# A change to the second block's attentions in a two-block transformer kernel: pairs of heads in one accumulator, another order on ScalarE, one joined head loop

## The reference

```
proj = rmsnorm(h) @ w_in[l];  main, mq = proj[..., :768], proj[..., 768:]
layer 0: main_out = pool_mixer(main)      # four groups, window means over 2, 4, 8, 16 tokens
layer 1: main_out = swa_sink_attention(rmsnorm(main), k_shared, v_shared, sinks)
         # 12 query heads of width 64, 4 key/value heads, window 128, causal, position bias,
         # a learned sink in each softmax's denominator
mem_out = memory_attention(rmsnorm(mq), mk, mv)          # 4 heads of width 64, 256 memory rows
h = h + concat([main_out, mem_out]) @ w_out[l]
h = h + relu(rmsnorm(h) @ w_up[l])**2 @ w_down[l]
```

## Time and profile before

| | us |
|---|---|
| median of 3 runs | 1760.87 (1757.15 to 1761.19) |
| the profiled execution, its own time | 1758.72 |
| its span, first to last instruction | 1756.9 |
| TensorE busy | 1525.0 (87%) |
| VectorE busy | 1062.1 (60%) |
| ScalarE busy | 754.9 (43%) |
| GpSimd busy | 276.7 (16%) |
| mean granted TensorE clock | 0.982 of full |

### The profile page before, as it was taken

One profiled execution on the slowest core, in us unless ns is written; L12 is line 12 of the kernel. 1 busy time (PEld: TensorE's weight loads), 2 busy tenths in 40 slices (PEclk: granted clock), 3 DMA queues, 4 the chain that ended last, 5 costly groups with the idle time before them and its releaser, 6 DMA issues.

```text
span 1756.9 us, 20895 instructions
## 1 busy us (share of the span) xinstructions
PE 1525.0 (87%) x8008; PEld 1145.7 (65%) x8008; DVE 1062.1 (60%) x1938; ACT 754.9 (43%) x1395; POOL 276.7 (16%) x326
## 2 busy tenths in 40 slices
PE   7999999998998877777777687777999999789999
PEld 7998989977883322222222232256899878679987
DVE  5468646764486667666677766456544556754454
ACT  5544555443443333334333333244455346545532
POOL 0000000000023343334333343303000002000000
PEclk9999999999999999999999999999999999899999
DMA  6744344453479999999999999942455653124563
GB/s 247 247 177 144 145 144 148 168 171 114 144 292 418 421 422 422 421 421 421 421 416 422 422 406 422 422 171 73 168 171 189 192 174 100 45 88 177 192 191 120
DMA packets 71043, 442.11 MB, mean 252 GB/s; under 512 B 7031, under 2 KB 9343, under 8 KB 25504
## 3 DMA queue, kind: packets, MB, share of 16 engines
q0 software_dynamic: 36864, 268.45, 36.9%
q1 hardware_dynamic: 30208, 163.59, 27.1%
q10 hardware_dynamic: 3872, 8.75, 1.4%
HBM read 439.70 MB, written 2.63 MB: 252 GB/s over the span
## 4 chain that ended last, share of the span: by engine, by line
PE 58%; DMA 24%; DVE 9%; ACT 5%; issue 2%; POOL 1%; ACTq 0%; SPq 0%; DVEq 0%; POOLq 0%
PE banks L1070 28%; DMA arena<-experts,xn 24%; PE banks L1099 16%; PE banks L1352 7%; DVE w_lo L1495 2%; DVE arena L1888 2%; PE banks L1196 1%; PE banks L1183 1%; PE banks L1136 1%; ACT xn L884 1%; ACT xn L888 1%; ACT w_hi L608 1%; ACT op_hi L633 1%; ACT xn L877 1%; ACT arena L687 0%
## 5 line engine op out<-in xcount | busy, mean ns | idle before, releaser
L1352 PE MATMUL banks<-arena,xn 128*128 128x512 f32 x1024 | 483.7, 618 | 157.4 <-ACT xn L888 157.4
L1495 DVE TENSOR_TENSOR w_lo<-raw,w_hi 128x2048 fp32r<-128x2048 f32 x154 | 352.3, 2290 | 261.6 <-PE banks L1070 131.7
L1352 PEld LDWEIGHTS banks<-arena,xn 128*128 128x128 f32 x1024 | 189.4, 194 | 449.6 <-ACT xn L888 256.0
L1888 DVE CUSTOM_DVE_ANT_0 arena<-arena,banks 128x1024 f32<-128x1024 f32 x256 | 312.1, 1219 | 213.6 <-DMA arena<-experts,xn 213.2
L608 ACT ACTIVATE w_hi<-raw 128x2048 fp32r<-128x2048 f32 x154 | 293.3, 1911 | 162.3 <-PE banks L1099 131.6
L546 POOL DMA_INDIRECT arena<-experts,xn x256 | 243.3, 950 | 435.9 <-PE banks L1352 383.8
L1070 PE MATMUL banks<-op_hi,w_hi 128*128 128x256 f32 x1520 | 220.5, 287 | 2.3 <-ACT op_hi L633 2.3
L1070 PE MATMUL banks<-op_hi,w_lo 128*128 128x256 f32 x1520 | 214.1, 284 | 7.8 <-DVE w_lo L1495 7.8
L1070 PE MATMUL banks<-op_lo,w_hi 128*128 128x256 f32 x1520 | 214.2, 284 | 0.0
L877 ACT ACTIVATE xn<-xn,stat 128x2 f32<-128x2 f32 x128 | 37.8, 295 | 395.1 <-DVE xn L1888 395.1
L1070 PEld LDWEIGHTS banks<-op_hi,w_hi 128*128 128x128 f32 x1520 | 198.2, 193 | 6.9 <-ACT op_hi L633 4.3
(11 more groups left out here) (225 smaller groups left out, 1154.1 us busy)
## 6 DMA issues: line engine op xcount, KB each, us to landing
raw<-wstream SPq DMA_DIRECT2D x154, 1024.0 KB, 5.1
arena<-experts,xn POOLq DMA_INDIRECT x256, 12.6
xn<-mem_in ACTq DMA_DIRECT2D x2, 1024.0 KB, 4.8
scratch<-scratch ACTq DMA_DIRECT2D x1, 1536.0 KB
x<-x_in SPq DMA_DIRECT2D x2, 512.0 KB, 4.3
arena<-scratch ACTq DMA_DIRECT2D x1, 1024.0 KB, 7.4
arena<-keys_in ACTq DMA_DIRECT2D x1, 1024.0 KB, 5.9
out_dram<-x SPq DMA_DIRECT2D x4, 256.0 KB, 2.0
```

What stands on the lines that cost most here:

```text
L1352: mm = pe.matmul(sums[:, n, :], diag[:, s, :], rows[:, s, D + n * CW:D + (n + 1) * CW], start=(at == 0), stop=(at == PAIRS - 1), skip_grou ...
L1495: dve.tensor_tensor(w_lo[:, n % LO, :, :], raw[:, n % RAW, :, :], w_hi[:, n % HI, :, :].bitcast(F32), ALU.subtract).then_inc(lo_ready, 1)
L1888: dve.tensor_tensor_reduce(u, u, token_rows[k // PAIRS][:, :, :], 1.0, 0.0, ALU.mult, ALU.add, dots[:, s:s + 1]).then_inc(dot_ready, 1)
```

## The change

There are five parts.

1. Two windowed heads share an accumulator. `v_swa` becomes `[P, TB, 2, 2, P]`: for each value head a tile with zeros to its right and one with zeros to its left (two memsets and two copies of half the width in place of one copy). The value products of heads 2p and 2p+1 add into one projection bank, and K is done once for the pair, on 128 partitions.
2. In the second layer's two loops ScalarE does C(i) ahead of E(i+2) in place of behind it.
3. The loops are joined: S, M and E of the first two memory heads are issued in the windowed loop at heads 10 and 11.
4. The last square root (memory queries) is gone from ScalarE: it adds 1e-6 and copies, and POOL raises to -0.5. VectorE only negates.
5. Pooling tile 5 goes from POOL to VectorE, behind M(3) of the first memory attention; the splits of blocks (0,0) and (0,1) follow it.

The diff, cut to its core:

```diff
 plan():
+        if c == "inb" and i:
+            for p in range(SWA_TILES):
+                place(lin, lin_uses, ("O", "swa", p))
 ...
+            elif after:
+                m("S", after, i + lag - items)
-            if i:
+            if i and kind != "swa":
                 m("O", kind, i - 1)
             m("T", kind, i)
-    attention("swa", SWA_HEADS, 1, 2, [("qr", 2)], [(), (), [("qr", 3)]])
-    attention("memb", MEM_HEADS, 1, 2)
+    attention("swa", SWA_HEADS, 1, 2, [("qr", 2)], [(), (), [("qr", 3)]], after="memb")
+    attention("memb", MEM_HEADS, 1, 2, begun=True)
-        v_swa = part(4608, TB, S)
+        v_swa = part(5632, TB, 2, 2, P)
 gpsimd:
-            for t in range(3, SWA_TILES):
+            for t in (3, 4):
 ...
+            misc_emptied(pool, ("qr", 3))
+            pool.tensor_tensor(query_inv[:, 3, :], query_root[:, 3, :], small[:, 14:15].broadcast_to([P, 8]), ALU.pow)\
+                .then_inc(memory_roots, 1)
 scalar:
-                if i >= 2:
+                if i >= 2 and kind == "swa":
+                    act.wait_ge(swa_out, i - 1)
+                elif i >= 2:
                     wait_misc(act, ("O", kind, i - 2))
 ...
                 for i in range(items):
+                    if kind in ("swa", "memb"):
+                        turned(kind, i)
                     if i + lag < items:
                         for g in range(group):
                             free_prob(kind, i + lag, group)
                             exps(kind, (i + lag) * group + g)
+                    elif after:
+                        free_prob(kind, i + lag, group)
+                        exps(after, i + lag - items)
 ...
-                    turned(kind, i)
+                    if kind not in ("swa", "memb"):
+                        turned(kind, i)
 ...
-            copy_lin(("kvb", 1), v_swa[:, :, :])
+            product(("kvb", 1))
+            act.wait_ge(v_zeros, 1)
+            v = lin_bank(("kvb", 1)).rearrange("p (t a c d) -> p t a c d", t=TB, a=2, c=2)
+            for c in range(2):
+                e = act.activation(v_swa[:, :, :, c, c * HD:(c + 1) * HD], v[:, :, :, c, :], ACT.Copy)
+            empty_lin(e, ("kvb", 1))
+            def memory_means():
+                key = ("qr", 3)
+                wait_misc(act, key)
+                empty_misc(act.activation(query_root[:, 3, :], misc_bank(key)[:, 0:8], ACT.Identity,
+                                          bias=small[:, 9:10]), key)
 tensor:
+                    if kind == "swa":
+                        key = ("O", "swa", i // 2)
+                        if i % 2 == 0:
+                            lin_bank_free(key)
+                        for kb in range(2):
+                            mm = pe.matmul(lin_bank(key)[:, kb * P:S], values(i)[0](kb),
+                                           prob_t[:, (ITEM0[kind] + i) % 2, kb * S:(kb + 1) * S - kb * P],
+                                           start=(i % 2 == 0 and kb == 0), stop=(i % 2 == 1 and kb == 1))
+                        mm.then_inc(swa_out, 1)
+                        return
 ...
+                    elif after:
+                        s(i + lag - items, *after)
-                      lambda u: [lambda kb: v_swa[:, kb, (u // 6) * P:(u // 6 + 1) * P]],
+                      lambda u: [lambda kb: v_swa[:, kb, u // 6, u % 2, :]],
 vector:
+                    if kind == "swa":
+                        if i % 2:
+                            key = ("O", "swa", i // 2)
+                            dve.wait_ge(swa_out, i + 1)
+                            src, t = lin_bank(key)[:, 0:S], i // 2
+                            do(dve.tensor_copy(op_hi[:, 1, t, :], src))
+                            empty_lin(dve.tensor_tensor(op_lo[:, 1, t, :], src, op_hi[:, 1, t, :].bitcast(F32),
+                                                        ALU.subtract), key)
+                        return
 ...
+            def last_window():
+                lin_emptied(dve, ("ina", 3))
+                windows(SWA_TILES - 1)
+                pool_low(0, 0)
+                pool_low(0, 1)
-                      [next_low_parts, pool_lows((0, 0), (0, 1)), pool_lows((0, 2), (1, 0)), pool_lows((1, 1), (1, 2))])
+                      [next_low_parts, last_window, pool_lows((0, 2), (1, 0)), pool_lows((1, 1), (1, 2))])
 ...
+            do(dve.memset(v_swa[:, :, :, 0, HD:P], 0.0))
+            dve.memset(v_swa[:, :, :, 1, 0:HD], 0.0).then_inc(v_zeros, 1)
 ...
+            def memory_inverses():
+                low_parts(LAST[("inb", 3)] + 2)
+                dve.wait_ge(memory_roots, 1)
+                do(dve.tensor_scalar(query_neg[:, 3, :], query_inv[:, 3, :], -1.0, None, ALU.mult))
```

More of the change, by code:

```diff
@@ L135, in norm, with attention @@
             m("xT", n, j)
-    def attention(kind, items, group, lag, between=(), fill=()):
-        for i in range(min(lag, items)):
+    def attention(kind, items, group, lag, between=(), fill=(), after=None, begun=False):
+        for i in range(0 if begun else min(lag, items)):
             for g in range(group):
@@ L345, in build @@
         late_windows = sem("late_windows")
+        memory_roots = sem("memory_roots")
+        swa_out = sem("swa_out")
+        v_zeros = sem("v_zeros")
         query_gains = sem("query_gains")
@@ L707, in free_prob, with attention @@
                     wait_misc(act, ("T", kind, j))
-            def attention(kind, items, group, lag, fill=(), between=None):
+            def attention(kind, items, group, lag, fill=(), between=None, after=None, begun=False):
                 start = halves[0]
-                for i in range(min(lag, items)):
+                for i in range(0 if begun else min(lag, items)):
                     for g in range(group):
@@ L1011, in _ @@
             query_roots(("qr", 1), 1)
-            attention("swa", SWA_HEADS, 1, 2, [None, None, lambda: query_roots(("qr", 3), 3)], last_queries)
-            attention("memb", MEM_HEADS, 1, 2)
+            attention("swa", SWA_HEADS, 1, 2, [None, None, memory_means], last_queries, after="memb")
+            attention("memb", MEM_HEADS, 1, 2, begun=True)
             squares_and_rows("mlpb", "outb", 0)
@@ L1172, in normed, with attention, s @@
                 return dict(hi_made=made(norm_hi), lo_made=made(norm_lo))
-            def attention(kind, items, group, lag, scores, values, fill=(), between=None):
-                def s(u):
+            def attention(kind, items, group, lag, scores, values, fill=(), between=None, after=None, begun=False):
+                def s(u, kind=kind, scores=scores):
                     b = fill_misc(("S", kind, u))
@@ L1452, in _, with memory_scores @@
             point(pe, "k_swa")
+            def memory_scores(h, qb):
+                if h == 0 and qb == 0:
+                    misc_emptied(pe, ("qr", 3))
+                return [(q_swa[:, h % 2, SWA_TILES + h // 2, qb * P:(qb + 1) * P], memk[:, 1, h // 2, :])]
             attention("swa", SWA_HEADS, 1, 2,
@@ L1455, in _ @@
                                      (slopes[:, u, qb, :], alibi[:, qb, :])],
-                      lambda u: [lambda kb: v_swa[:, kb, (u // 6) * P:(u // 6 + 1) * P]],
-                      [None, None, lambda: query_means_b(3)], last_half)
-            misc_emptied(pe, ("qr", 3))
-            attention("memb", MEM_HEADS, 1, 2,
-                      lambda h, qb: [(q_swa[:, h % 2, SWA_TILES + h // 2, qb * P:(qb + 1) * P],
-                                      memk[:, 1, h // 2, :])],
-                      lambda h: [lambda kb: memv[:, 1, kb, (h // 2) * P:(h // 2 + 1) * P]])
-            for u in range(SWA_HEADS):
-                misc_emptied(pe, ("O", "swa", u))
+                      lambda u: [lambda kb: v_swa[:, kb, u // 6, u % 2, :]],
+                      [None, None, lambda: query_means_b(3)], last_half, after=("memb", memory_scores))
+            attention("memb", MEM_HEADS, 1, 2, memory_scores,
+                      lambda h: [lambda kb: memv[:, 1, kb, (h // 2) * P:(h // 2 + 1) * P]], begun=True)
+            for p in range(SWA_TILES):
+                lin_emptied(pe, ("O", "swa", p))
             for h in range(MEM_HEADS):
@@ L1654, in normalise, with attention @@
                                       ALU.mult).then_inc(p_ready, 1)
-            def attention(kind, items, group, lag, extra, dst, fill=(), lows=()):
-                for i in range(min(lag, items)):
+            def attention(kind, items, group, lag, extra, dst, fill=(), lows=(), after=None, begun=False):
+                for i in range(0 if begun else min(lag, items)):
                     for g in range(group):
@@ L1684, in attention @@
                             maxima(kind, u, **extra(u))
+                    elif after:
+                        wait_misc(dve, ("T", kind, i + lag - 4))
+                        maxima(after, i + lag - items)
                     if i < len(lows):
@@ L1992, in windows @@
```

(8 more changed lines are left out.)

4 lines of the change are left out of this document (2 added, 2 removed).

## The result

| | us |
|---|---|
| changed kernel, median of 6 runs | 1743.9 (1741.1 to 1748.0) |
| kernel before, beside it, median of 6 | 1758.7 (1754.8 to 1761.2) |
| ratio, with its 95% interval | 0.9917 (0.9899 to 0.9936) |
| profiled execution, its span | 1741.14, 1739.3 |
| forecast, range | 1744.9, 1739.5 to 1752 |

The change saves 14.8 us by the medians, where 16.0 were forecast.

The account below looks back on a forecast made before the run. Head stages were taken as round trips between engines, VectorE nearest to full. 3.7 + 3.0 + 4.7 + 1.1 - 0.3 + 3.8 = 16.0 us saved gave 1742.7, or 1744.9 us on the runs' scale; range 1739.5 to 1752.

Parts of the forecast that it names:

- What bounds the kernel: Second layer's head stages: a round trip between engines, VectorE nearest to full; a microsecond saved there is saved at the end.
- The loop: Steady windowed heads, N(4) to N(11): K once per pair lowers VectorE's work; 3.0 us gain, bounds 0 to 3.7.
- about nothing: Steady loop under the new bank rules: S(i+3)'s wait for E(i+1) was judged to cost about nothing.
- Rival E: Windowed loop: VectorE's work isn't the limit, 2.95 us per head stays; 3.0 less gain, 1747.9 us; chance 12%.
- The first heads: N(1) to N(4): table loads and a bank wait go, N(4) starts earlier; 3.7 us gain, bounds 1.5 to 4.5.
- The joint: End of N(11) to end of memory head 0's N: 8.5 us becomes 3.8; 4.7 gain, bounds 3.5 to 5.5.
- The memory heads: Memory head 0's N to the output projection: 11.9 us becomes 10.8; 1.1 gain, between 0 and 2.
- Copies and memsets: Ahead of the loop: two copies in place of one cost 0 to 0.6 us, taken as -0.3.
- Pooling: Layer 0, tile 5 on VectorE: block (1,0) starts earlier despite half collision; 3.8 us gain, bounds 0.5 to 6.3.
- rival D: Layer 0's pooling: VectorE and POOL collide fully, gain 0.5 in place of 3.8 us, 1748.2 us; chance 12%.
- Rival B: Shortened loop: TensorE's clock falls for half of seven steps, costing 4.9 us, 1749.8 us; chance 15%.
- rival C: Clock stays low from N(1) through the memory heads and beside the pooling: 4.6 us slower, 1765.5 us; chance 3%.

Follow-up runs that it names:

- e4: Changed kernel with K done twice for each pair (same values written again); median 1749.47 us, ratio 0.995.
- e2: Changed kernel with part 2 undone, ScalarE doing E(i+2) ahead of C(i) again; median 1748.12 us, ratio 0.9945.
- e10: Part 1 alone on the kernel before, the other four parts undone; median 1753.76 us, ratio 0.9975.
- e5: Part 2 alone on the kernel before, C(i) ahead of E(i+2); median 1758.5 us against 1759.02, ratio 1.0002.
- e11: Changed kernel with part 4 undone, the memory queries' square root on ScalarE again; median 1742.76 us, ratio 0.991.
- e3: Changed kernel with part 3 undone, windowed and memory heads as two loops again; median 1746.71 us, ratio 0.993.
- e8: Changed kernel with K of the last windowed pair moved behind N and M of memory head 0; median 1742.24 us, ratio 0.991.
- e9: Changed kernel with that K moved later and the first heads' `low_parts` moved behind the memory heads; median 1741.59 us, ratio 0.991.
- the changed kernel's second profile: The changed kernel run again without edits, beside later runs; median 1746.43 us, ratio 0.9929.

## Why the prediction held, step by step

**What bounds the kernel.** The reading that a microsecond saved in the stages is one saved at the end held: the stage gains sum to 14.6, the medians differ by 14.8, and from the projection to the end both profiles took 209.6. The time came out 1.0 from the forecast, nearer than the saving (14.8 for 16.0), because the kernel before, measured beside it, was 2.1 lower than the median that the forecast started from. That is luck, and so is part of the sum: the loop gave 0.9 more than forecast, the first heads 1.45 and the pooling 0.9 less.

**The loop** (3.0 forecast, 3.93 measured). VectorE is the bound, as said, and e4 shows it. The forecast without hand-offs was 17.1, and 16.72 came: a pair took the 4.78 worked out, and the first and the last step were shorter, 2.67 and 2.61 for 2.78. So the 0.5 that I kept for hand-offs was not needed. What failed is the step that gave the gain to part 1 alone. It compared busy times of single engines and found S's wait for E "about nothing". It did not follow the ring through ScalarE's list, where C stood behind E: 5.73 us per pair in e2 and in the middle of e10. Rival E had the right suspicion (the loop keeps 2.95, C comes through two engines), and its own counter, "C moves ahead", is half of the answer. Part 2 opens this ring, but alone it closes the one through E's bank, 3.20 per head in e5; part 1, which moves O out of those banks, opens that one and lowers VectorE's own work besides. With both rings open VectorE's list is what is left. So neither part shows without the other (20.09 and 21.20 alone).

**The first heads** (3.7, 2.25). The term that was mis-sized is the clock at S(4), which I had in the bounds (1.5 to 4.5) and at zero in the sum: it took 1.66. Where it did not occur (e11), the stretch was 9.81, and 13.49 - 9.81 is the forecast's 3.7. The kernel before had run this stretch at 0.87, so at like clocks the new order is worth 2.25. Counting the two table loads among the causes was wrong in attribution: e11 has them and loses 0.23.

**The joint** (4.7, 4.75). Length and chain as worked out. But the forecast compared a stretch of the changed kernel at full clock with one of before at 0.68, and put all of it on the joining, which is worth 1.9 (e3). Another 1.9 belong to the clock and the order of C together (e5); no run parts these two. So the near match of 4.7 and 4.75 is partly luck.

**The memory heads** (1.1, 0.86). It is part 2's: 11.05 to 11.07 in every profile with C first but three, 11.92 in those without (before, e2, e10). The three are e4, at a clock of 0.84, and e8 and e9, which have K of the last pair in this stretch.

**Copies and memsets** (-0.3, -0.1). From the pooling stage to N(1), where no stretch was slow, 261.09 against 261.01 in e5, which lacks them. The two memsets took 0.27 each.

**Pooling** (3.8, 2.9). The collision was sized at half and was larger: tile 5 took 5.9 us, not 5.1, and POOL's tile 4 beside it 1.0 more than alone. The splits behind it kept their length (0.86 for two, 0.87 before). It was not rival D's 8 us. The Trainium skill, GPSIMD Engine Reference, section Specifications, says that POOL shares its SBUF interfaces with VectorE and contends with instructions of VectorE that have two SBUF inputs or run in a two-port mode. The trace agrees for the two-input ones (0.42 became 0.63 and 0.80), but not each was stretched: the additions that VectorE began together with a copy of POOL kept 0.42. Copies, with one input, were caught as well: 0.60, 0.60 and 0.71 for two, four and eight columns, while that of one column kept 0.14 beside POOL's addition. In which mode these copies ran the trace does not tell.

**Rival B and rival C** (the clock falls in the loop, or everywhere). Neither occurred: 1.00 in loop, joint and memory heads. In e10 the clock was 0.87 in the loop and 0.61 in the joint, so the danger was real for half of this change. The Trainium skill, TensorE: Matmul & The Clock Gate, section A second HAM failure mode: psum-queue depth-cycling, which the prediction named for B, says that short pauses between groups of products, as banks cycle, can make the clock swing. No run here shows it: e10's middle pairs, with waits of 0.2 to 0.4 us in front of O in every head, ran at 0.99 and 1.00, as the changed kernel's loop did at 1.00, and e10's clock was low where TensorE had waited 1.5 us and more.

**The prices of rivals B and C.** C's own terms add to 4.1 + 0.3 = 4.4, where 4.6 was written, and B took 1.75 for the lower level where its row gives 634/379 = 1.67. Neither changes the outcome.

**The rest of the spans' 17.6.** The stages of these two profiles give 14.1. The other 3.5 lie in stretches that no part touches: 1.85 ahead of the pooling stage, whose cause is open, and 1.6 between it and N(1). There every profile has about 261.1, 262.6 or 264.3, steps of 1.6. One such step, the transposes ahead of layer 1's projections, in the kernel before:

```profile
1438.30:1450.40 12.10, 11.45 (x82) 11.28 (x83) 9.51 (x20) 6.86 (x17) 0.00 (x0) 0.86 0.31 108
```

The same 82 products take 11.45 us busy here at a granted 0.86, and 9.82 in the changed kernel at 1.00 (the second row of its windows above). Both occur with the same kernel: the changed kernel's second profile has 264.3 in the larger stretch. Such steps may well be the 2.5 us between its own two medians, 1743.9 and 1746.4, but that is not shown, since only one execution of each was profiled. What decides whether such a stretch comes slow was not found.

## What to carry to other kernels

In a loop that goes head by head over in-order engines, compare each engine's work per round with the longest ring of waits through all the lists and banks, over as many heads as banks and buffers span. An instruction that stands behind another on a half-idle engine can close a ring that hides a gain elsewhere, and moving it can close the next ring, so two edits may be worth 3.9 us together and 1.4 apart. A mean per head over a short loop can hide a ring, so read the steps one by one. Before crediting a stretch to an edit, read its granted clock on both sides. An elementwise piece moved to the neighbour of a busy engine costs more than its own time: here 5.9 us for 3.5, and 1.0 to the other.

## What was new about the hardware

- GpSimd's power over 128x8 took 1.65 us in both profiles quoted, against 0.54 to 0.72 for one or two columns.
- VectorE and POOL beside each other take turns, and the shortest instructions pay: a copy of four columns took 0.60 on VectorE, where one or two columns alone take 0.15 to 0.17, and 0.47 for 0.19 on POOL.
- A fall of TensorE's clock lengthened a stretch by about the same time each time: 1.63 in the transposes, 1.66 at S(4), 1.66 more in the first heads of the second profile. In unchanged work it came in some executions of one kernel and not in others.
